# A four-layer f32 decoder on one Trainium2 core: the delta rule's inverse rebuilt from one masked factor per level without GpSimd, and the last layer's side work set out anew by ticks

## What is computed

```python
def odd_layer(x, ...):
    proj = rmsnorm(x, norm_g) @ w_in
    xc, zc, qd, kd, vd, zd, a_pre, b_pre = split_cols(proj, OD_SIZES)
    xconv = causal_dwconv(xc, conv_c_w) + conv_c_b            # four taps
    yc = rg_lru(xconv, gate_w, gate_b, lam) * silu(zc)
    qkv = silu(causal_dwconv(concat([qd, kd, vd]), conv_d_w))  # four taps
    q, k = l2norm(q), l2norm(k)
    od = gated_delta_chunkwise(q, k, v, beta, g)
    yd = rmsnorm(od, onorm_g) * silu(zd)
    return concat([yc, yd]) @ w_out

    # inside gated_delta_chunkwise
    a_mat = where(strict, einsum(kbeta, kc) * gam, 0)
    t_inv = triangular_solve(eye + a_mat, eye)
    u = t_inv @ (vc * bc)
```

## Time and profile before

| what | value |
|---|---|
| median of 3 runs (lowest to highest) | 2554.68 us (2554.19 to 2555.42) |
| the profiled execution's own time | 2554.72 us |
| its span | 2553.0 us |
| PE busy in the span | 2479.8 us (97%) |
| DVE, ACT, POOL busy | 1425.8, 1217.7, 184.6 us |
| mean granted PE clock | 0.989 |

### The profile page before, as it was taken

One profiled execution on the slowest core, in us unless ns is written; L12 is line 12 of the kernel. 1 busy time (PEld: TensorE's weight loads), 2 busy tenths in 40 slices (PEclk: granted clock), 3 DMA queues, 4 the chain that ended last, 5 costly groups with the idle time before them and its releaser, 6 DMA issues.

```text
span 2553.0 us, 30128 instructions
## 1 busy us (share of the span) xinstructions
PE 2479.8 (97%) x12030; PEld 2065.3 (81%) x12030; DVE 1425.8 (56%) x1881; ACT 1217.7 (48%) x1644; POOL 184.6 (7%) x171
## 2 busy tenths in 40 slices
PE   8999999999999999989999989999999999999889
PEld 6888888888888888868887868888888878788777
DVE  5545464646464555555545565554545566666674
ACT  4444444444444445344555454554444455444453
POOL 1101010101010100000000000000000012212100
PEclk9999999999999999989999989999999999999999
DMA  7545455555555554535433545555555553333344
GB/s 239 191 153 194 160 180 170 167 182 174 171 181 167 165 182 173 194 123 194 161 104 119 196 153 185 180 165 185 173 173 175 176 178 118 109 106 116 99 131 133
DMA packets 350240, 414.49 MB, mean 162 GB/s; under 512 B 19018, under 2 KB 285476, under 8 KB 349588
## 3 DMA queue, kind: packets, MB, share of 16 engines
q1 hardware_dynamic: 348692, 405.63, 49.5%
q0 software_dynamic: 1408, 6.94, 0.7%
HBM read 410.42 MB, written 2.10 MB: 162 GB/s over the span
## 4 chain that ended last, share of the span: by engine, by line
PE 90%; DVE 5%; ACT 3%; issue 1%; POOL 0%; DMA 0%; SPq 0%; ACTq 0%; DVEq 0%
PE ps L545 26%; PE ps L547 26%; PE ps L546 26%; PE ps L585 2%; PE ps L959 2%; PE ps L700 1%; DVE wlo L1630 1%; ACT whi L1097 1%; DVE work L2099 1%; PE ps L687 1%; PE ps L761 1%; PE ps L692 1%; PE ps L760 1%; PE ps L773 0%; PE ps L684 0%
## 5 line engine op out<-in xcount | busy, mean ns | idle before, releaser
L1630 DVE TENSOR_TENSOR wlo<-raw,whi 128x1024 fp32r<-128x1024 f32 (+1 forms) x774 | 954.4, 1239 | 840.0 <-ACT whi L1097 837.8
L545 PE MATMUL ps<-whi,xh 128*128 128x512 f32 (+1 forms) x3072 | 1228.7, 400 | 7.4 <-DVE wlo L1630 7.4
L547 PE MATMUL ps<-whi,xl 128*128 128x512 f32 (+1 forms) x3072 | 1198.1, 390 | 0.0
L546 PE MATMUL ps<-wlo,xh 128*128 128x512 f32 (+1 forms) x3072 | 1196.6, 390 | 0.0
L1097 ACT CAST whi<-raw 128x1024 fp32r<-128x1024 f32 (+1 forms) x774 | 801.6, 1041 | 803.0 <-PE ps L547 798.8
L545 PEld LDWEIGHTS ps<-whi,xh 128*128 128x128 f32 x3072 | 579.7, 189 | 124.8 <-issue 12.1
L547 PEld LDWEIGHTS ps<-whi,xl 128*128 128x128 f32 x3072 | 578.4, 188 | 121.1
L546 PEld LDWEIGHTS ps<-wlo,xh 128*128 128x128 f32 x3072 | 579.6, 189 | 110.2
L2375 POOL TENSOR_TENSOR work<-work 128x512 f32<-128x512 f32 x48 | 77.1, 1606 | 872.6 <-DVE work L1815 488.6
L1175 ACT ACTIVATE work<-work,small 128x128 f32<-128x128 f32 (+1 forms) x80 | 46.1, 577 | 155.7 <-DVE small L1740 155.7
L959 PEld LDWEIGHTS ps<-work 128*128 128x128 f32 x544 | 68.2, 193 | 16.7 <-issue 7.0
(11 more groups left out here) (371 smaller groups left out, 1403.6 us busy)
## 6 DMA issues: line engine op xcount, KB each, us to landing
raw<-in_dsa_w_in SPq DMA_DIRECT2D x320, 512.0 KB, 4.5
raw<-in_ev_w_in SPq DMA_DIRECT2D x144, 512.0 KB, 4.6
raw<-in_od_w_in SPq DMA_DIRECT2D x96, 512.0 KB, 4.5
raw<-in_mla_w_in SPq DMA_DIRECT2D x48, 512.0 KB, 4.3
raw<-in_dsa_w_out SPq DMA_DIRECT2D x32, 512.0 KB, 4.5
raw<-in_mla_w_out SPq DMA_DIRECT2D x32, 512.0 KB, 4.7
raw<-in_ev_w_out SPq DMA_DIRECT2D x32, 512.0 KB, 4.5
raw<-in_od_w_out SPq DMA_DIRECT2D x32, 512.0 KB, 4.8
```

The source lines that it names most:

```text
L545: pe.matmul(o, xh[:, k, tokens[tb]], hi, start=start and s + l == 0, stop=False)
L546: pe.matmul(o, xh[:, k, tokens[tb]], lo, start=False, stop=False)
L547: m = pe.matmul(o, xl[:, k, tokens[tb]], hi, start=False, stop=stop and s + l == 2)
L1630: dve.tensor_tensor(whole_half(wlo[:, h % 4], n), whole_half(raw[:, h // 2 % 4, 2 * (h % 2):2 * (h % 2) + 2], n), whole_half(whi[:, h % 4] ...
```

## The change

Six things are changed, all in the last layer.

1. The masks `lev` get the sign -1 and the identity. `AD` gets ones on its diagonal from one affine select on POOL. `AD * lev` is then identity minus the masked part, so that a level is: z = `AD` by `Mt` on PE, one masked copy `Z` out of PSUM on DVE, t = `M` by `Z` and d = `Z` by `M` on PE, and two plain copies to `Mt` and `M` on ACT. POOL has no work in the levels.
2. v's convolution is three taps on DVE. The first tap of every convolution (q, k, v and the RG-LRU's) is now a scaled copy on ACT.
3. A step of `delta` is one tick, and its steps are numbered anew (96 instead of 61). A level takes 6 ticks instead of 8.
4. The transposes of v, the decays and the products have other places: `e` and the scalars `rb`, `c2`, `rq` come ahead of `u`.
5. The lanes start at other ticks.
6. `EARLY[3]` is 6: one more block of `y` is transposed inside the last projection, and none behind the first unit of `last_product`.

```diff
-EARLY = (6, 4, 6, 5)
+EARLY = (6, 4, 6, 6)
...
-    lane = [[(0, 1, gates()), (66, 2, delta(0)), (194, 2, delta(2)), (317, 1, lru(0)), (346, 1, lru(1)), (376, 1, lru(2))],
-            [(130, 2, delta(1)), (258, 2, delta(3)), (382, 1, lru(3))]]
+    lane = [[(0, gates()), (68, delta(0)), (196, delta(2)), (293, lru(0)), (326, lru(1)), (359, lru(2))],
+            [(132, delta(1)), (260, delta(3)), (363, lru(3))]]
...
             def delta(pair):                       # PE
-                yield from to(11)
+                yield from to(20)
                 pe.wait_ge(*da.at(r, "sq"))
...
-                yield from to(19)
+                yield from to(30)
                 pe.wait_ge(*dd.at(r, "u"))
...
                 for l in range(1, 7):
-                    yield from to(25 + 4 * l)
-                    pe.wait_ge(*dg.at(r, f"b{l}"))
-                    pe.wait_ge(*(da.at(r, "mt") if l == 1 else dd.at(r, f"mt{l - 1}")))
-                    four_by_four(b, v.B, v.Mt).then_inc(*dp.up(f"z{l}"))
-                    yield from to(27 + 4 * l)
-                    pe.wait_ge(*da.at(r, f"z{l}"))
+                    yield from to(38 + 6 * l)
+                    pe.wait_ge(*da.at(r, f"mt{l - 1}"))
+                    four_by_four(b, v.AD, v.Mt).then_inc(*dp.up(f"z{l}"))
+                    yield from to(41 + 6 * l)
+                    pe.wait_ge(*dd.at(r, f"z{l}"))
                     if l > 1:
-                        pe.wait_ge(*dd.at(r, f"m{l - 1}"))
-                    m = four_by_four(b, v.M, v.Z)
+                        pe.wait_ge(*da.at(r, f"m{l - 1}"))
+                    four_by_four(b, v.M, v.Z).then_inc(*dp.up(f"t{l}"))
                     if l < 6:
-                        m = four_by_four(b + 1, v.Z, v.M)
-                    m.then_inc(*dp.up(f"d{l}"))
...
             def delta(pair):                       # ACT
-                yield from to(17)
+                yield from to(26)
                 act.wait_ge(*dd.at(r, "e"))
...
             def delta(pair):                       # DVE
+                for step, what, *args in ((3, conv, 0, 1), (5, conv, 0, 2), (7, conv, 0, 3), (9, conv, 1, 1), (11, conv, 1, 2),
+                                          (12, silu, 0), (14, conv, 1, 3), (16, conv, 2, 1), (17, silu, 1), (19, conv, 2, 2)):
                     yield from to(step)
...
+                yield from to(28)
                 dve.wait_ge(*dp.at(r, "vt"))
                 dve.tensor_tensor(v.u.rearrange("p h t d -> p (h t) d"), ps[:, b + 1, :].rearrange("p (k d) -> p k d", k=4),
                                   bc(sc[:, 8:12], 2, P), ALU.mult).then_inc(*dd.up("u"))
...
                 for l in range(1, 7):
-                    yield from to(27 + 4 * l)
-                    dve.wait_ge(*dp.at(r, f"d{l}"))
-                    if l > 1:
-                        dve.wait_ge(*dd.at(r, f"m{l - 1}"))
-                    dve.tensor_tensor(flat(v.Mt), flat(v.Mt), ps[:, b, :], ALU.subtract).then_inc(*dd.up(f"mt{l}"))
-                    if l < 6:
-                        dve.tensor_tensor(flat(v.M), flat(v.M), ps[:, b + 1, :], ALU.subtract).then_inc(*dd.up(f"m{l}"))
+                    yield from to(38 + 6 * l)
+                    dve.wait_ge(*dp.at(r, f"z{l}"))
+                    dve.tensor_tensor(v.Z, ps[:, b, :].rearrange("p (k d) -> p k d", k=4), bc(L3.lev[:, l], 1, 4),
+                                      ALU.mult).then_inc(*dd.up(f"z{l}"))
...
             def delta(pair):                       # POOL
-                for l in range(7):
-                    yield from to(22 if l == 0 else 23 + 4 * l)
-                    pool.wait_ge(*(dd.at(r, "ad") if l == 0 else dd.at(r, "m") if l == 1 else dp.at(r, f"z{l - 1}")))
-                    pool.tensor_tensor(v.B, v.AD, bc(L3.lev[:, l], 1, 4), ALU.mult).then_inc(*dg.up(f"b{l}"))
+                yield from to(34)
+                pool.wait_ge(*dd.at(r, "ad1"))
+                pool.affine_select(out=v.AD, in_=v.AD, compare_op=ALU.not_equal, fill=1.0, base=0,
+                                   pattern=[[0, 4], [-1, P]], channel_multiplier=1).then_inc(*dg.up("diag"))
```

More of the change, by code:

```diff
@@ L95, in lanes @@
 def lanes(gates, delta, lru):
[L99 to L100 removed]
+    lane = [[(0, gates()), (68, delta(0)), (196, delta(2)), (293, lru(0)), (326, lru(1)), (359, lru(2))],
+            [(132, delta(1)), (260, delta(3)), (363, lru(3))]]
     tick = 0
     while lane[0] or lane[1]:
[L103 to L107 removed]
+        for side in lane:
+            if side and tick >= side[0][0] and next(side[0][1], "over") == "over":
+                del side[0]
         tick += 1
@@ L974, in delta @@
                 m.then_inc(*dp.up("ss"))
[L975 to L977 removed]
+                yield from to(23)
                 pe.wait_ge(*dd.at(r, "eps"))
@@ L2183, in delta, with conv, silu @@
-                yield from to(12)
+                KINDS = (("q", v.QT), ("k", v.KT), ("v", v.VT))
+                def conv(n, j):
+                    kind, dst = KINDS[n]
+                    dve.wait_ge(*(dd.at(r, f"{kind}{j - 1}") if j > 1 else da.at(r, kind + "0")))
+                    for hh in range(2):
+                        m = tap(j, dst[:, hh], v.cpd[:, 2 * n + hh], vcol("cd", 1, 24 * j + 8 * n + 2 * pair + hh))
+                    m.then_inc(*dd.up(kind + "012c"[j]))
+                def silu(n):
+                    kind, dst = KINDS[n]
+                    dve.wait_ge(*dd.at(r, kind + "c"))
+                    dve.wait_ge(*da.at(r, "th" + kind))
+                    dve.scalar_tensor_tensor(out=flat(dst), in0=v.tanh[n], scalar=1.0, in1=flat(dst),
+                                             op0=ALU.add, op1=ALU.mult).then_inc(*dd.up("s" + kind))
@@ new lines, in delta @@
+                yield from to(24)
+                silu(2)
+                yield from to(25)
+                dve.wait_ge(*dp.at(r, "r"))
+                rows_ = ps[:, b, :].rearrange("p (h t) -> p h t", h=2)
+                mask = bc(L3.mincl, 1, 2)
+                dve.tensor_tensor(sc[:, 20:22], rows_[:, :, P - 1], L3.dcol[:, 1, 2 * pair:2 * pair + 2], ALU.add).then_inc(*dd.up("td"))
+                dve.scalar_tensor_tensor(out=v.E[:, :, 0:P], in0=rows_[:, :, 0:P], scalar=-1.0, in1=mask, op0=ALU.mult, op1=ALU.add)
```

294 lines of the change are left out of this document (130 added, 164 removed).

## The result

The changed kernel takes 2573.93 us (median of 4 runs, 2572.39 to 2575.18) where the kernel before takes 2554.93 on the same chip (4 runs): a ratio of 1.0074, with a 95% interval from 1.0057 to 1.0092. It is slower by 19.0 us. The profiled execution took 2573.76 us, with a span of 2572.0 us and a mean granted clock of 0.985.

What follows compares the result with a forecast made beforehand. PE was taken as the bound, side work mattering where results come late for its tick. The kernel before's 2554.7 us plus 17 of waits plus 4 of clock gave 2575.7, rounded to 2575; own range 2562 to 2583, whole range 2546 to 2589.

Steps and rivals of the forecast that it cites:

- kk for u: PE's step 30, once a pair: K's products wait for DVE's `u`, four waits of 3.6 us or more, 18.4 us.
- ss of the first pair: Step 20, tick 88: PE waits 4.5 us for the first sums of squares, 1.0 before for the third transposes.
- Tick 320: Boundary with two gates: PE's t4 waits 2.8 us behind DVE's two gates, a split and the masked copy.
- Tick 384: Boundary with two gates: PE waits for the scan 6.1 us, up to 9.6 if ACT is late; 7.2 taken.
- The small ones: Waits for copies of u, `qk` for `AD`, other output steps and v's transposes: 12.1 us in all.
- The waits together: All PE waits in the last layer: 46.0 us against 29.0 before, so +17.0.
- The clock: Lower clock behind seven waits of 2.7 us or more, 1.7 each: 11.9 instead of 7.9 us, +4.0.
- the clock pays: Rival: waits as forecast, each long one costs 3.2 us of clock, +14.5, about 2586 us; chance 0.08.
- nothing, if the lower clock falls into the waits: Lower alternative for the clock behind PE's long waits: no added cost instead of +4.0 us.
- Arithmetic as such: DVE about 2 us lighter a pair from changed subtractions, masked copies and taps; PE's own work the same.
- POOL: No wait of PE for POOL, POOL under 15 us busy in the layer, DVE's taps near 485 ns.
- faster, because the queues are quieter: Rival: lighter DVE, old waits go and none come, about 2533 us; holds if `kk` waits under 1 us; chance 0.18.

Runs made afterwards that it cites:

- Experiment 1: Changed kernel with DVE's `u` one step earlier, ahead of the split: 2558.11 us, ratio 1.0011.
- experiment 10: The version of experiment 8 with `u` behind the four instructions of `e` and a step later, PE's ticks unchanged: 2542.31 us, ratio 0.9949.
- Experiment 2: Changed kernel with the scan's transposes and `end` of lru(2) and lru(3) 8 steps later on every engine: 2568.54 us, ratio 1.0051.
- Experiment 11: Changed kernel with `EARLY` back at (6, 4, 6, 5): 2573.45 us, ratio 1.0072.
- Experiment 5: Kernel of experiment 3 with scans 6 more steps later, u's first copy one step earlier, delta(0)'s steps from 20 on four ticks later: 2552.84 us, ratio 0.9997.
- Experiment 3: Changed kernel with the edits of experiments 1 and 2 together: 2552.63 us, ratio 0.9990.
- experiment 8: Kernel before's ticks, lanes and order with the new inverse and q, k, v convolutions; `EARLY` 5, RG-LRU first taps on DVE: 2542.28 us, ratio 0.9951.
- Experiment 4: Kernel before with the new inverse alone (masked copies on DVE, plain copies on ACT), its own ticks and convolutions: 2553.72 us, ratio 0.9997.
- experiment 6: Changed kernel with six unused 128x512 products a pair on POOL at the levels' ticks: 2578.58 us, ratio 1.0090.
- experiment 9: The version of experiment 8 with lru(3) started at tick 386 in place of 382: 2542.3 us, ratio 0.9951.

## Why the prediction was right, step by step

The forecast was 2575.0 us, the measurement 2573.93. The mechanism held: the waits that were named came at the places named. Its two sizes were off in opposite directions, PE's idle time over-sized by 6.2 us (+17.0 said, +10.8 measured) and its clock under-sized by 4.3 (+4.0 said, +8.3 of busy time measured). That the sum came within 1.1 us of the measured time is in part luck.

*kk for u*: 18.4 forecast, 16.7 measured, as 3.4, 4.9, 3.5 and 4.9 for 3.8, 5.3, 4.0 and 5.3. Two of the four are a little below the "3.6 us or more" of the prediction. The chain in the timeline is the one that was summed, name by name. Experiment 1 shows the cause; experiment 10 shows that the place behind `e` and a split alone does not make it.

*ss of the first pair*: 4.5 + 1.0 forecast, 3.9 + 0.6 measured. *Tick 320*: 2.8 forecast, 2.5 measured (the row of 2.8 has a second wait of 0.4).

*Tick 384*: 7.2 forecast out of 6.1 to 9.6, 9.7 measured, 8.8 of it in one. From the first gate instruction to the end of the scan it is 8.7 us (2470.81 to 2479.47), against 8.8 in the prediction's chain. What was wrong is the start. It gave PE four ticks, 2.7 us, before PE asks, but PE asks at 2470.7, when ACT has not begun the gates. ACT comes to them late, behind a table load and the square root of the RG-LRU:

```profile
2468.98 1.28 ACT L1505 ACT_TABLE_LOAD   x1
...
2470.28 0.63 ACT L1505 ACTIVATE work<-work 128x512 f32<-128x512 f32 x1
...
2470.81 0.82 ACT L1585 ACTIVATE y<-ps,hrstd 128x256 f32<-128x256 f32 x2
...
2471.64 1.28 ACT L1589 ACT_TABLE_LOAD   x1
```

The load at 2471.64 stands within the gates, and the kernel before has one there too (2450.95), so it is in the 4.6 us of the prediction. The prediction named first taps, casts and table loads as what could make ACT 3.5 us late; the upper end of its range had this, and the value taken did not. Experiment 2 shows that the wait depends on the tick at which PE asks: 8 ticks took 5.4 us off it.

*The small ones*: 12.1 forecast, 7.0 measured (4.4 for the copies of u, which had 6.0; 1.2 for `qk`, which had 1.6; and 1.4 where 4.5 stood for the rest). This was the most over-sized term. It had been put together from guesses of 0.3 to 1.0 for operations that mostly didn't wait at all.

*The waits together*: 46.0 forecast, 40.7 measured; +10.9 over the 29.8 of before, where +17.0 was said.

*The clock*: this is the step that was sized wrong the other way: +4.0 forecast, +10.3 measured in lost clock, of which +6.0 while PE was busy, and +8.3 in PE's busy time. The number of long waits, seven, was right: they end at 2100.8, 2117.9, 2198.3, 2278.2, 2358.7, 2404.2 and 2479.5 us. But the price of 1.7 each, read from three of four stretches in the earlier trace rows, was too small. The lost clock at each was either about 1.7 (three of them) or about 3.4 (four: the 3.9 at 2100.8, both waits of 4.9, and the 8.8), which a single stretch of 10 us often shows only half of. That makes 18.8. Where the lower clock fell into the wait, PE lost less: about 2.3 of the 3.4 at the two waits of 4.9, and 1.7 of the 3.4 at the 8.8. So the cost lies between the forecast's +4.0 and the +14.5 of the rival "the clock pays", and the prediction's "nothing, if the lower clock falls into the waits" is right for 4.5 of the 18.8 us.

The Trainium skill (TensorE: Matmul & The Clock Gate, HAM oscillation) says that each gap can cost the ramp again. The trace agrees that it is paid again at each of seven waits of 2.5 us or more, the smaller price behind waits of 2.5, 3.4 and 3.5 us. In the kernel before, the wait of 2.5 cost 3.4 (3.2 of them in the stretch shown) and those of 4.0, 3.7 and 1.9 about 1.7. What decides was not found, and the length of the wait is not it. Experiment 11 has 5.1 around a wait of 8.7 us where the changed kernel has 3.4 around one of 8.8. Experiment 5 has 5.2 in the 20 us from 2100 on, behind a wait of 1.2 us. Experiment 3 has 1.7 between 2170 and 2190, where the longest wait is 1.0.

*Arithmetic as such*: "about -2 us a pair" for DVE and nothing for PE. Here the prediction saw too little. By experiment 8 the delta rule's arithmetic is worth 12.8 us in the old ticks. The time goes from before to after as -12.8 for that and +31.7 for the rest, where the prediction had booked it as waits gone and waits new in one sum. The rest is the order by ticks, `EARLY` (nothing, by experiment 11) and the RG-LRU's first taps on ACT, which no run has alone; experiment 3 gives 21.3 of the 31.7 to two places of the order. The sum came out, the parts were never told apart.

*POOL*: no wait of PE for it, as said; 15.6 us busy against "under 15". The taps are at 480 ns, as said. Experiment 4 shows that 59 of the 124 ns between were the masks'. The other 65 are most likely v's sums, beside which six taps of experiment 4 took 3.62 us instead of 2.72. Where POOL has no such work, in the changed kernel, no tap took more than 490 ns, and in the kernel before the longest took 1555. By the Trainium skill (SBUF — State Buffer, Who interferes with whom) a VectorE instruction with two SBUF inputs contends with a GpSimd instruction that reads SBUF, and the lock is exclusive. In experiment 6 POOL's 40.1 us lengthen DVE's instructions by 5 to 7, an eighth to a sixth. So no run here shows the full exclusion over all of POOL's time. Single instructions show something near it: beside POOL's products one split of experiment 6 took 2.20 us, where none takes more than 1.23 without them, and POOL's products themselves took from 1.27 to 2.31.

*The rivals*: "faster, because the queues are quieter" was said to decide at `kk`; experiment 1 took that wait away and came to 2558.1, not to 2533, since the scan's wait and four others of 2.8 us or more in total stayed. The affine select and `EARLY` were costed at nothing, rightly (no row of PE behind either, experiment 11).

Why experiment 5 gained nothing over 3 can be read from the same two sums: its waits are 22.2 us in all instead of 24.9, and its lost clock is 13.8 instead of 10.2, so -2.7 and +3.6, against medians that are 0.2 us apart. The additional lost clock is in three places: 1.8 us more around 2100, although the wait there fell from 3.9 to 1.2; 1.7 around 2200, behind the wait of 3.9; and 3.5 around 2255, at a wait of 1.4, where experiment 3 has 1.7 near 2274. The wait for the scan near 2465 and its 1.7 are gone.

What stays open: what makes the lost clock at a wait 1.7, 3.4 or 5.1 us; what the RG-LRU's first taps on ACT are worth; how the 16.7 us at `kk` divide between the distance in ticks and the scaling between the casts; and whether an order faster than that of before exists for the new arithmetic; experiment 9 was the only step there that moved anything but `u`.

## What to carry to other kernels

When side work runs in order beside a bound engine, price a move by what stands ahead of the result in its queue, other engines' work that this queue waits for included, against the ticks until it is asked for; here 0.69 us of work, four times behind a split, cost 16 us. Time a new arithmetic in the old order before judging either: here it gave 12.8 us, and what was changed on top, nearly all of it order, took 31.7. After the large waits are gone, moving a single step by ticks can move the wait to the next request of the same queue, as in experiment 9, where the queue itself was no shorter.

## What the runs showed of the hardware

The lost clock at a wait of PE came in sizes of some 1.7, 3.4 and 5.1 us, and not in proportion to the wait: 3.4 at one of 8.8 us and at one of 3.9 in the changed kernel, 5.1 at the same wait of 8.7 in experiment 11. A part of it can lie within the wait, where it costs nothing: of the 18.8 us of the changed kernel 4.5. A table load took ACT 1.28 us, and the gate and the recurrence exchange tables three times within 9 us (2468.98, 2471.64 and 2476.32). VectorE's taps took 474 to 490 ns with POOL free of products and sums and up to 1555 beside them. On POOL a power of 128x8 took 1.81 us and one of 128x4 1.10, more than a sum of 128x256 with its 0.93, while an affine select of 128x512 took 0.64.
